# A hybrid decoder layer: where TensorE turns attention weights around for the first of two PSUM banks

## The reference

```
h = _rms_norm(x, norm_mix[l])
proj = h @ w_in[l].astype(h.dtype)            # q | k | v | B | C | u
...
z = jnp.einsum('bhqd,bhkd->bhqk', q_blk.astype(jnp.float32), k32) * scale
causal = key_pos[None, :] < q_pos[:, None]
sp = jax.nn.softplus(z)
neg_log_rem = jnp.where(causal, sp, 0.0)
after = lax.cumsum(neg_log_rem, axis=3, reverse=True) - neg_log_rem
log_a = (z - sp) - after
a = jnp.where(causal, jnp.exp(log_a), 0.0)
return jnp.einsum('bhqk,bhkd->bhqd', a, v32)
...
conv = _short_conv_mixer(cb, cc, cu, conv_w[l])   # B * conv_w3(C * u), causal, width 3
x = x + jnp.concatenate([attn, conv], axis=-1) @ w_out[l]
x = x + (jax.nn.silu(h2 @ w_gate) * (h2 @ w_up)) @ w_down
```

## The kernel before

| slot | blocks scored | steps | fills (of unit n-3) |
|---|---|---|---|
| 8 | 4 | 1 | 2 |
| 12 / 13 | 5 / 8 | 4 / 0 | 2 / 2 |
| 14 | 6 | 3 | 2 |
| 16 | 3 | 2 | 2 |
| 18 / 19 | 7 / 8 | 3 / 0 | 2 / 1 |
| 23 / 24 | 2 / 1 | 1 / 1 | 2 / 2 |
| 32 | 4 | 2 | 2 |
| 36 / 37 | 5 / 8 | 4 / 0 | 2 / 2 |
| 38 | 6 | 4 | 2 |
| 39 / 40 | 8 / 3 | 2 / 1 | 2 / 2 |

## Time and profile before

### The profile page before, as it was taken

The page is one execution under the profiler, slowest core; times in us unless marked ns, Lnnn a source line. Parts: engine busy times, 40 slices in busy tenths (PEclk is TensorE's granted clock), DMA queues, the critical chain, the costliest instruction groups (busy, mean ns, idle before and its releaser), DMA issues.

```text
span 2660.5 us, 34870 instructions
## 1 busy us (share of the span) xinstructions
PE 2518.8 (95%) x12272; PEld 2082.3 (78%) x12272; DVE 1303.8 (49%) x1315; ACT 1139.8 (43%) x1857; POOL 1239.7 (47%) x865
## 2 busy tenths in 40 slices
PE   8999879999899999799799999999999999999999
PEld 6788657777777777678678888888887888888887
DVE  4433346776676677534564544432534545442222
ACT  3222256766676677432343333322433333332322
POOL 1212156767667676301375544423486455442332
PEclk9999989999999999899899999999999999999999
DMA  5665573343533522254422122256543222214554
GB/s 174 192 186 158 159 195 98 109 131 99 145 90 94 157 73 66 89 166 143 158 80 94 60 83 95 94 165 207 190 145 101 95 71 79 87 63 154 166 190 154
DMA packets 299865, 336.03 MB, mean 126 GB/s; under 512 B 17888, under 2 KB 239072, under 8 KB 298720
## 3 DMA queue, kind: packets, MB, share of 16 engines
q1 hardware_dynamic: 299744, 334.57, 41.0%
HBM read 240.13 MB, written 94.37 MB: 126 GB/s over the span
## 4 chain that ended last, share of the span: by engine, by line
PE 48%; POOL 1%; DMA 1%; DVE 0%; ACT 0%; issue 0%; SPq 0%; ACTq 0%; DVEq 0%
PE ffn_ps L1791 10%; PE ffn_ps L1793 10%; PE ffn_ps L1795 10%; PE ffn_ps L76 6%; PE ffn_ps L77 6%; PE ffn_ps L78 6%; POOL ffn_A L1731 1%; DMA ffn_raw<-in_w_up 1%; ACT ffn_A L1461 0%; DVE ffn_raw L1601 0%; DVE ffn_raw L1611 0%; DVE ffn_raw L1606 0%; DVE ffn_s L1647 0%; DVE ffn_s L1597 0%; ACT ffn_s L1473 0%
## 5 line engine op out<-in xcount | busy, mean ns | idle before, releaser
L1731 POOL TENSOR_TENSOR ffn_A<-ffn_raw,ffn_A 128x512 fp32r<-128x512 f32 x264 | 364.7, 1392 | 379.0 <-ACT ffn_A L1461 378.7
L1791 PE MATMUL ffn_ps<-all_B,ffn_A 128*128 128x512 f32 x1232 | 481.3, 391 | 17.9 <-POOL ffn_A L1731 15.8
L1793 PE MATMUL ffn_ps<-all_B,ffn_A 128*128 128x512 f32 x1232 | 480.7, 390 | 0.0
L1795 PE MATMUL ffn_ps<-all_B,ffn_A 128*128 128x512 f32 x1232 | 480.6, 390 | 0.0
L829 DVE TENSOR_TENSOR_SCAN att_stick<-att_z,att_stick 128x128 f32<-128x128 f32 (+5 forms) x192 | 331.2, 1726 | 221.8 <-ACT att_z L741 210.5
L875 POOL TENSOR_TENSOR att_a<-att_a,att_stick 128x128 f32<-128x128 f32 (+5 forms) x192 | 281.6, 1472 | 215.3 <-DVE att_stick L829 214.5
L1736 POOL TENSOR_TENSOR ffn_A<-ffn_A_over,ffn_A 128x512 fp32r<-128x512 f32 x88 | 160.3, 1821 | 333.7 <-ACT ffn_A L1494 333.7
L1791 PEld LDWEIGHTS ffn_ps<-all_B,ffn_A 128*128 128x128 f32 x1232 | 232.3, 189 | 67.4 <-POOL ffn_A L1731 19.1
L1639 DVE TENSOR_TENSOR ffn_A<-ffn_A_over,ffn_A 128x1024 fp32r<-128x1024 f32 x88 | 117.3, 1333 | 322.2 <-ACT ffn_A L1492 322.2
L76 PE MATMUL ffn_ps<-ffn_A 128*128 128x512 f32 x704 | 273.9, 389 | 0.0
L77 PE MATMUL ffn_ps<-ffn_A 128*128 128x512 f32 x704 | 273.9, 389 | 0.0
(11 more groups left out here) (122 smaller groups left out, 5035.7 us busy)
## 6 DMA issues: line engine op xcount, KB each, us to landing
ffn_A_over<-in_w_down SPq DMA_DIRECT2D x88, 512.0 KB, 3.5
att_w_stage<-in_w_in SPq DMA_DIRECT2D x48, 512.0 KB, 4.4
ffn_raw<-in_w_gate SPq DMA_DIRECT2D x22, 1024.0 KB, 6.7
ffn_raw<-in_w_up SPq DMA_DIRECT2D x22, 1024.0 KB, 8.8
hidT<-ffn_s SPq DMA_DIRECT2D x88, 256.0 KB, 2.4
ffn_A_over<-hidT SPq DMA_DIRECT2D x88, 256.0 KB, 3.7
qkv_x_t<-in_x SPq DMA_DIRECT2D x16, 512.0 KB, 4.5
hT_hi<-qkv_hT_hi SPq DMA_DIRECT2D x16, 512.0 KB, 5.4
```

The source lines that it names most:

```text
L1731: nc.gpsimd.tensor_tensor(A[:, j, p, 1, :, :], operand(j, p), A[:, j, p, 0, :, :].bitcast(F32), ALU.subtract).then_inc(lo_done, 1)
L1791: nc.tensor.matmul(ps[:, b, :], A[:, j, p, 0, k, :], B[p][:, 0, k, :], start=first_mm, stop=False, skip_group_check=True)
L1793: nc.tensor.matmul(ps[:, b, :], A[:, j, p, 0, k, :], B[p][:, 1, k, :], start=False, stop=False, skip_group_check=True)
L1795: mm = nc.tensor.matmul(ps[:, b, :], A[:, j, p, 1, k, :], B[p][:, 0, k, :], start=False, stop=last_mm, skip_group_check=True)
```

## The change

`transposes` gets a third argument. With 0 it fills all banks of the unit but the last, with 1 the last. In the body of a slot, part 0 stands right behind the scores, ahead of the steps, for a unit with two fills (for one with a single fill it isn't called); part 1 stands where `transposes` stood. The other engines' programs are not changed, nor is the order of the fills among themselves. The three slots behind the last pair call both parts one behind the other, as before.

```diff
-            def transposes(p, n):
+            def transposes(p, n, part):
+
                 p, n = at(p, n)
                 gi, h, t, j0, nb = units[n]
                 pe.wait_ge(a_done, NU * p + n + 1)
-                for f in range(fills[n], fills[n + 1]):
+                split = fills[n + 1] - 1
+                for f in range(fills[n], split) if part == 0 else range(split, fills[n + 1]):
                     wait(pe, aT_lo_done, FILLS * p + f - 1)
                     j = 4 * (f - fills[n])
                     for i in range(min(4, nb - j)):
...
                 for n in range(NU):
                     scores(p, n)
+                    lagging = n >= LAG or not is_first(p)
+                    if lagging and fills[at(p, n - LAG)[1] + 1] - fills[at(p, n - LAG)[1]] > 1:
+                        transposes(p, n - LAG, 0)
                     for k, i in steps[n]:
                         project_step(p, k, i)
-                    if n >= LAG or not is_first(p):
-                        transposes(p, n - LAG)
+                    if lagging:
+                        transposes(p, n - LAG, 1)
                     q, b = at(p, n - LAG)
                     if opens[b] and (n > LAG or not is_first(p)):
                         a_times_v(q, units[b][0] - 1)
 
             pairs(pe, body)
             for n in range(NU - LAG, NU):
-                transposes(PAIRS - 1, n)
+                for part in range(2):
+                    transposes(PAIRS - 1, n, part)
```

## The result

| | before | after |
|---|---|---|
| median of 4 runs, us | 2660.53 | 2682.28 |
| lowest, highest | 2657.15, 2662.24 | 2679.60, 2686.57 |
| ratio | | 1.0085, 95% interval 1.0066 to 1.0103 |
| profiled execution: span | 2660.5 | 2678.4 |
| attention stage, first to last matmul | 337.3 to 1103.8 | 336.5 to 1123.7 |

The change makes the kernel 21.75 us slower by the medians; 2683 was forecast. The two profiled executions lie only 17.9 us apart: the stage is 20.7 us longer (787.2 instead of 766.5), and the rest gives back 2.8, of which 0.8 ahead of the stage and 2.0 behind it, where no instruction was changed. What gives it back isn't shown; one wait of TensorE for POOL in the feed-forward part is 1.3 us shorter there.

What follows compares the result with a forecast made beforehand. TensorE was taken to bound the attention stage. Slot terms of 5.95 us a pair times 4 gave 23.8, less 1.9 for switching: +21.9 us on 2662.36, 2684.3; with the median 1.2 lower the forecast was 2683, range 2672 to 2696.

Steps and rivals of the forecast that it cites:

- The bound: Attention stage: TensorE, busy 697 of 765 us, sets the pace; whatever makes it idle lengthens the stage.
- Slots 8, 14, 32 and 38: Moved fills that now wait for their bank: +0.33 us a pair in slot 8, +1.20, +1.22 and +1.20 in the others.
- The cause of the late bank: DVE's subtraction that frees the bank stands behind its slot's scan, which takes 2.35 us for eight blocks.
- Waits that change places: Slots 15, 17, 18, 41, 42: bank late by 0.5 to 0.65 us, but offset by neighbouring slots' waits; zero net.
- rival 3: The waits add up: slots 15, 17, 18, 41, 42 pay too, 2.8 x 4 = 11 us more, 2694; chance 0.06.
- Net +1.47: Slot 16, us a pair: a new wait of 2.15 for the bank, less old waits of 0.43 and 0.25 that vanish.
- rival 4: The clock: two more half-clock drops a pair, 8 x 4 = 32 us more, 2715; chance 0.03.
- Slots 36 and 37: POOL finishes the product 0.02 us after the steps began, so the early fill gains nothing; 0, bounds -0.66 and +0.5.
- Slots 23 and 24: New waits for the bank in both slots, partly offset by old waits that vanish: +0.40 us a pair.
- 39 and 40: Slot 39's fill covers 0.44 us of waiting for ACT, slot 40 then waits 1.37 for its bank: +0.79 a pair.
- Switching: First step matmul behind the mask matmul costs 0.09 us more; a fill between saves 0.04 in 12 slots a pair: -1.9.
- the sum of 21.9: Whole change: 5.95 us a pair times 4 pairs = 23.8, less 1.9 for the matmul behind the mask: +21.9 us.

Runs made afterwards that it cites:

- run 8: Kernel before, without the change, with the same 96 steps of a pair distributed over the slots by another fixed table: 2612.75 us, -47.9 us.
- run 1: Kernel before with the first bank filled ahead of the steps only in the eight late-bank slots (8, 14, 16, 23, 24, 32, 38, 40): 2687.95 us, +27.8.
- run 2: Kernel before with the first bank filled early only in ten slots whose bank is in time (4, 6, 10, 12, 21, 28, 30, 34, 36, 45): 2655.14 us, -5.0.
- run 5: Changed kernel, with DVE's subtraction of the first of two fills moved ahead of the scan of its slot: 2672.87 us, +12.3 against the kernel before.
- run 6: Changed kernel with DVE's first subtraction ahead of the scan and ACT's first copy ahead of the sigmoids: 2659.51 us, -1.1 against the kernel before.
- run 3: Kernel before with the first bank filled ahead of the steps in slot 16 alone: 2669.33 us, +9.2 us.
- run 4: Kernel before with, in slot 16 alone, the first bank filled behind the first of its two steps: 2662.09 us, +1.9 us.
- run 7: Changed kernel with the first bank filled behind the first step instead of behind the scores, in all 24 slots: 2668.95 us, +8.3 against the kernel before.

## Why the prediction was right

**The bound.** TensorE's idle time in the stage grew by 20.6 us, its busy time and that of all others stayed. That it sets the pace is also what run 8 shows from the other side.

**The waits.** Slots 8, 14, 32 and 38 cost within 0.15 us of the forecast, but for slot 8 in pair 0, which cost nothing. Reading three times beside each other in the trace of before (scores through, bank free, steps begun) was enough. Runs 1 and 2 separate the two kinds of slots: +27.8 and -5.0 sum to +22.8, close to the whole change's +21.75, so the six slots that are in neither run come to about nothing together.

**The cause of the late bank.** Shown by runs 5 and 6: the subtraction's place behind the scan, then the copy's place behind the sigmoids. With both moved, TensorE's wait at the fills is 31.1 us, under the 34.8 of the kernel before.

**Waits that change places.** Slots 18 with 19 and 41 to 43 came out at nought within 0.05 us, and slots 15 and 17 by themselves at -0.01 to -0.21, so rival 3's addend does not exist.

**Slot 16 was mis-sized.** "Net +1.47" left the clock out; +2.8 to +3.1 was measured in three pairs, +1.53 in the one that kept its clock. That is rival 4's mechanism at one place a pair instead of two, and a third of its price each time: 1.4 us instead of 4, some 4 us in all instead of 32. I had argued that stops of up to 2.2 us would leave the clock alone because the "many stops of one to two us" between 600 and 700 did. That reading was wrong: the window holds two of at least one us, 1.02 us in slot 24 and this one in slot 22:

```profile
621.03 1.12 PE L965 MATMUL att_tr<-all_ident,att_a 128*128 128x128 f32 x8 [1.49 <-DVE att_aT_lo L841]
```

Outside pair 0's first slots and the loop's turn the longest stop in the whole stage is 1.65, so no row of that trace says what the clock does behind stops of 2 us. Runs 3 and 4 show that one of 1.94 us here often did not leave the clock alone, and one of 0.78 did.

**Slots 36 and 37 were mis-sized too.** "I take 0, by the POOL row": -0.45 to -0.56 was measured. The row was right and the conclusion was not. Slot 32 ahead of it now loses 1.1 us, and POOL, which does not wait with TensorE, catches up:

```profile
673.34 2.00 POOL L875 TENSOR_TENSOR att_a<-att_a,att_stick 128x1024 f32<-128x1024 f32 x1
675.78 0.61 PE L967 MATMUL att_tr<-all_ident,att_a 128*128 128x128 f32 x4
676.51 0.47 PE L76 MATMUL att_proj<-att_hT_hi,att_w_hi 128*128 128x512 f32 x1
```

The product ends at 675.34, ahead of the scores' end, where before it ended 0.8 us behind it. Run 2, in which slot 32 does not wait, has its four waits of 0.6 at this place, and its slots 36 and 37 together gain 0.1 to 0.2 instead of 0.5. Slots 23 and 24 (+0.63 instead of +0.40) and 39 and 40 (+0.61 instead of +0.79) are off by less, and opposite.

**Switching** was forecast at -1.9, for 12 slots a pair without a new wait. There are 11, and 8 of them have the mask, so the same price gives -1.3. The 11 slots of the table's last line (8 with a moved fill, and 5, 9 and 29 with a single fill) came out some 0.5 a pair shorter, about 2 us in all. Pair 0's -0.93 is left out of that: 0.35 of it, in slots 4 and 5, is there in run 3 too, which moves nothing in them.

So the sum of 21.9 is right partly by luck, because its errors cancel: 4 us too few for the clock and 1 for slots 23 and 24, against some 2 too many for slots 36 and 37, 0.7 for slots 39 and 40, 0.7 for slot 25, for which it had no term, and the rest in small terms. The mechanism is right nearly slot by slot; the total is better than its parts.

## What to carry to other kernels

An instruction that waits for another engine should stand behind work that is ready, and the work between the producer's start and the wait is what pays for the latency: here moving the wait ahead of its cover cost the full difference, though no work was added. Lay the three times (arrival, resource free, start of the work that gets blocked) beside each other per slot before moving anything, and move only where the first is later than the second: the same edit gave -5 us in ten slots and +28 in eight. And where the order inside a slot has been tuned out, look at how much cover each slot gets: here giving 96 equal steps another distribution was worth ten times the best reordering (-47.9 against -5.0 us).

## What was not expected of the hardware

- TensorE's clock fell to half for 3.4 us behind stops of only 1.9 to 2.2 us in slot 16 (three of four pairs in the changed kernel and in run 3, two of four in run 1) and cost about 1.4 us each time. The length of the stop does not settle it: of the changed kernel's two longest, 2.17 us in pair 0 and 2.16 in pair 3, the first kept its clock and the second did not, and in run 1 it was the other way round. The eight stops of 1.5 to 1.65 us in slots 22 and 46 of the kernel before passed at full clock, but for one shortly ahead of the loop's turn; in runs 2, 3, 6 and 7 one more of the eight, of 1.5 to 1.65 us and always in slot 46, was followed within 5 us by a stretch of 3.4. The Trainium skill ("TensorE: Matmul & The Clock Gate", "A second HAM failure mode: psum-queue depth-cycling") describes small stops between matmul groups that make the clock swing; here the trace agrees for stops of this size, most often for those of about 2 us.
- By the clock's records the stretch behind slot 16 of pair 1 begins at 599.2, 0.1 us before the fill that ends the stop: the stop itself loses nothing. The four transposes and the six step matmuls behind it do: the steps start 0.77 us behind the fill instead of 0.41 (run 4), and their matmuls follow 0.43 us apart instead of 0.23.
